# Latent attention of a fused two-block network: the former item's values ahead of this item's turns, ScalarE's copy between the two exponentials, the first low part at the tenth item

## The chip, the cores and the metric

One core of a Trainium2 chip. The time is device microseconds (us) for one execution of the whole program. TensorE (PE) multiplies and transposes into PSUM, VectorE (DVE) and ScalarE (ACT) read PSUM and SBUF, GpSimd (POOL) works on SBUF, and SyncE (SP) issues most transfers. Each engine runs its own list of instructions in order and waits on semaphores for the others.

## The reference

Two blocks work on 512 tokens of width 1024. The first block has two layers; each of them projects the normed input, runs a latent attention and a dilated attention, gates both, and adds a product with `w_out`. The second block has a feed-forward part, a recurrence with a banded attention, and another feed-forward part. The change lies in the latent attention, once in each of the two layers:

```python
q = (rms_norm(c_q, q_norm_g) @ w_uq).reshape(B, S, 8, 64 + 32)      # nope | rope
kv = (rms_norm(c_kv, kv_norm_g) @ w_ukv).reshape(B, S, 8, 64 + 64)  # k_nope | v
s = (einsum('bqhd,bkhd->bhqk', qn, k_nope) + einsum('bqhr,bkr->bhqk', qr, k_rope)) * 96 ** -0.5
p = softmax(s, axis=-1)
a = einsum('bhqk,bkhd->bqhd', p, v) * silu(gate_a)
x = x + concatenate([a, b], axis=-1) @ w_out
```

There is no mask: 8 heads, 512 queries, 512 keys.

## The kernel before

Large products run with both operands split into a high and a low part (three matmuls at lines 1208 to 1210), so nearly all of TensorE's time is such triples. Loads, splits and products follow a plan made when the program is built (`make_plan`).

**Items.** The latent attention (`kind == "mla"`) of a layer is cut into 16 items: item n has a pair of heads j = n // 4 and a tile of 128 queries t = n % 4. `first` marks t = 0 and `last` marks t = 3. Dilated and banded attention are cut the same way (`"dil"`, `"swa"`), and share the loops. `scores(n)` on TensorE makes 10 matmuls with 64 contracted rows for two heads side by side, over 512 keys, into two PSUM banks. DVE's `maxima(n)` reduces each bank (line 2617). ACT's `exp_of_item(n, parts)` takes the exponential of each bank into `PR` and sums it (line 1948); part 0 and part 1 are the two heads. `turn(n)` on TensorE transposes the probabilities into banks 4 and 5 (32 small transposes, line 1387; the first 16 need part 0, the others part 1). DVE copies bank 4 to `PT` (line 2635) and ACT copies bank 5 (line 1973, `turned(n)`). `values(n)` multiplies `PT` with the values into bank 6 (32 matmuls with 64 weight columns, line 1419).

**Buffers.** `PR` and `PT` hold two items each; banks 4 and 5 hold one. So `turn(n)` waits until both copies of item n-1 are done (`pt_dve`, `pt_act`), and `values(n)` waits for both copies of item n.

**After a pair of heads.** Behind a last item DVE takes the reciprocals of the sums (`sums_spread`, line 2641), ACT widens them (`sums_wide`, line 2007), TensorE transposes them into bank 7 (`spread_sums`, line 1400), and DVE multiplies the gate by bank 7 (line 2650) and by the values in bank 6 (line 2653, `result`). ACT then writes the high part of this product (`hi_of_value`, line 1991, in `CATM`) and DVE the low part (`lo_of_value`, line 2664). Both are operands of the output projection that follows the attention (`wo`, the triples on `CATD` and `CATM`). DVE also stacks low parts of later heads at items 0 to 3, 6 and 7 of the stage (`stack_low`, line 2706).

**Order before.** TensorE, for the latent attention: `scores(n+1)`, `turn(n)`, `spread_sums(n-1)` where item n-1 is a last one, `values(n-1)`. For the other attentions (`ahead`): `scores(n+1)`, `values(n-1)`, `turn(n)`. ACT, latent: both exponentials of item n+1, the copy of item n, the widening, the high part. ACT, other: exponential part 0, copy, result, exponential part 1. DVE: maxima of n+1, the copy of n, stacking, reciprocals, result of n-1, and a low part at items 6, 13 and 14 of the stage. The last two items are finished inside the first output projection (`rest`), in both versions alike.

Of the kernel before, what the change touches and what calls it, by code (L numbers as in the profile page):

```python
# [360 lines left out]
def build_program(nc, a, out):  # L361

    pl = make_plan()
    ctx = ExitStack()
    with ctx:
# [827 lines left out]
        def _(pe):  # L1193
# [160 lines left out]
            def attention(name, filler):  # L1354

                n0, n1 = pl.item_at[name]
                kind = name[0]
# [34 lines left out]
                def spread_sums(n):  # L1392

                    it = pl.items[n]
                    g = 4 * it["L"] + it["j"]
                    pe.wait_ge(rl_ready, g + 1)
                    if g:
                        pe.wait_ge(gated_a, g)
                    for t in range(NT):
                        last = nc.tensor.transpose(bank(7)[:, t * P:(t + 1) * P],  # L1400
                                                   RLB[:, 2 * t:2 * t + 2, :].rearrange("p h d -> p (h d)"), IDN[:, :])
                    last.then_inc(rlt_ready, 1)

                def values(n):
                    it = pl.items[n]
                    pe.wait_ge(pt_dve, n + 1)
                    pe.wait_ge(pt_act, n + 1)
                    if it["first"]:
                        results_taken(n)
                    if n == n0:  # L1410
                        if kind == "swa":
                            pe.wait_ge(dve_out, pl.dve_out[filler_of[name]])
                        elif kind == "dil":
                            pe.wait_ge(dve_out, pl.dve_out[filler_of[name]])
                            pe.wait_ge(w0_in if it["hh"] else v0_in, 16 * 12 * (it["L"] + 1))
                        else:
                            pe.wait_ge(act_out, pl.act_out["uv", it["L"], 1])
                    for dst, k, v, start, stop in value_products(it):
                        last = nc.tensor.matmul(dst, v, turned_block(n, k), start=start, stop=stop,  # L1419
                                                skip_group_check=True)  # L1420
                    last.then_inc(pv_done, 1)
# [7 lines left out]
                for n in range(n0, n1 - 1):  # L1429
                    if n0 + 1 < n + 1 < n1:  # L1430
                        scores(n + 1)
                    if ahead and n > n0:
                        values(n - 1)
                    turn(n)
                    if not ahead and n > n0:
                        if pl.items[n - 1]["last"]:
                            spread_sums(n - 1)
                        values(n - 1)

                def rest(k):  # L1440
                    if k == (1 if ahead else 5):
# [391 lines left out]
        def _(act):  # L1833
# [103 lines left out]
            def exp_of_item(n, heads=(0, 1)):  # L1937
                it = pl.items[n]
                kind, t, j = it["kind"], it["t"], it["j"]
                for b in heads:  # L1940
                    act.wait_ge(nm_ready, 2 * n + 1 + b)
                    if n >= 2:
                        act.wait_ge(t_ready, 2 * n - 3 + b)
                    sc = bank(2 * pl.pair["item", n] + b)
                    pr = PR[:, n % 2, b * S:(b + 1) * S]
                    if kind == "mla":
                        h = 2 * j + b
                        last = nc.scalar.activation(pr, sc, ACT.Exp, bias=NMM[:, h, t:t + 1], scale=1.0,
                                                    accum_out=LSM[:, h, t:t + 1])
                    elif kind == "dil":  # L1950
                        hh, h = it["hh"], 2 * it["jj"] + b
                        nc.scalar.activation(pr[:, 0:2 * P], sc[:, 0:2 * P], ACT.Exp,
                                             bias=NAT[:, hh, 0, 0, t, h:h + 1], scale=-1.0,
                                             accum_out=NAT[:, hh, 1, 0, t, h:h + 1])
                        last = nc.scalar.activation(pr[:, 2 * P:], sc[:, 2 * P:], ACT.Exp,
                                                    bias=RES[:, hh, t, 0, h:h + 1], scale=-1.0,
                                                    accum_out=RES[:, hh, t, 1, h:h + 1])
                    else:
                        w = min(t + 1, 2) * P
                        for u in range(2):  # L1960
                            h = 4 * j + 2 * u + b
                            last = nc.scalar.activation(pr[:, u * 2 * P:u * 2 * P + w], sc[:, u * 2 * P:u * 2 * P + w],
                                                        ACT.Exp, bias=SNM[:, h, t:t + 1], scale=-1.0,
                                                        accum_out=SLS[:, h, t:t + 1])
                    last.then_inc(p_ready, 1)

            def turned(n):

                act.wait_ge(t_ready, 2 * n + 2)
                if n >= 2:  # L1970
                    act.wait_ge(pv_done, n - 1)
                it = pl.items[n]
                nc.scalar.activation(used_half(it, PT[:, n % 2, S:]), used_half(it, bank(5)), ACT.Copy
                                     ).then_inc(pt_act, 1)

            def result(it):

                act.wait_ge(pv_done, it["n"] + 1)
                dst = OUN[:, it["j"], 1, :] if it["kind"] == "dil" else OSU[:, 2 * it["j"] + 1, :]
                nc.scalar.activation(dst, bank(7), ACT.Copy).then_inc(o_act, 1)  # L1980
# [29 lines left out]
            def attention(name, filler):  # L2010
                n0, n1 = pl.item_at[name]
                mla = name[0] == "mla"
                if not mla:
                    table(ACT.Exp)
                exp_of_item(n0)
                exp_of_item(n0 + 1)
                filler()
                for n in range(n0, n1):
                    more = n0 + 1 < n + 1 < n1
                    if more:  # L2020
                        exp_of_item(n + 1, (0, 1) if mla else (0,))
                    turned(n)
                    if mla and pl.items[n]["last"]:
                        sums_wide(pl.items[n])
                    if n > n0 and pl.items[n - 1]["last"] and not mla:
                        result(pl.items[n - 1])
                    if more and not mla:
                        exp_of_item(n + 1, (1,))
                    if n > n0 + 1 and pl.items[n - 2]["last"] and mla:
                        hi_of_value(("mla", name[1], pl.items[n - 2]["j"]))  # L2030
                if mla:
                    hi_of_value(("mla", name[1], HEADS // 2 - 1))
                else:
                    result(pl.items[n1 - 1])
                act.wait_ge(w_hi, pl.chunk[filler_of[name]] + 3)
# [412 lines left out]
        def _(dve):  # L2448
# [210 lines left out]
            def lo_of_value(key):  # L2659

                kind, L, j = key
                dve.wait_ge(cat_hi, pl.val[key])
                cat, src = (CATM, GA) if kind == "mla" else (CATD, GB)
                tt(cat[:, j, 1, :], src[:, j, :], cat[:, j, 0, :].bitcast(F32), ALU.subtract).then_inc(cat_lo, 1)
# [45 lines left out]
            def attention(name, filler=None):  # L2710
                n0, n1 = pl.item_at[name]
                mla = name[0] == "mla"
                maxima(n0)
                maxima(n0 + 1)
                if filler:
                    filler()
                for n in range(n0, n1):
                    it = pl.items[n]
                    if n0 + 1 < n + 1 < n1:
                        maxima(n + 1)  # L2720
                    turned(n)
                    if mla and heads_to_stack(name, n):
                        stack_low(name, heads_to_stack(name, n))
                    if mla and it["last"]:
                        sums_spread(it)
                    if n > n0 and pl.items[n - 1]["last"]:
                        result(pl.items[n - 1])
                    if mla and n - n0 in (6, 13, 14):
                        lo_of_value(("mla", name[1], (6, 13, 14).index(n - n0)))
                result(pl.items[n1 - 1])  # L2730
                if mla:
                    lo_of_value(("mla", name[1], HEADS // 2 - 1))
                dve.wait_ge(w_split, pl.chunk[filler_of[name]] + 3)
# [679 lines left out]
```

## Time and profile before

| what | value |
|---|---|
| median of 3 runs | 2043.9 us (2043.89 to 2044.02) |
| profiled execution, its own time | 2043.58 us |
| its span in the trace | 2041.8 us |
| PE busy | 2022.4 us, 99% |
| DVE, ACT, POOL busy | 1323.6, 911.6, 130.2 us |
| latent attention, layer 1, steady part | 363.97 to 407.92 us of the span |
| latent attention, layer 2, steady part | 806.27 to 850.23 us of the span |

The steady part runs from the start of the scores of item 2 to the start of the output projection. The profiled execution took 1.8 us more than its span, which lies around the first and last recorded instruction. A line of the timeline has the start of a group of like instructions, how long the group lasted, engine, line of the kernel, operation, destination and sources, shape and count; in brackets stands idle time ahead of it. Matmuls are pipelined: the start of the next group tells more than the length of one.

### The profile page before, as it was taken

The page shows a single profiled execution, that of the slowest core. Times are in us where ns is not written, and L with a number is a line of the kernel's source. Part 1 is how long each engine was busy: PE and PEld are TensorE (multiplying, and loading weights), DVE is VectorE, ACT ScalarE, POOL GpSimd, SP SyncE. Part 2 cuts the span into 40 slices and gives each one's busy share as a digit, 9 for nine tenths or more (in the row PEclk, how much of TensorE's full clock was granted, in tenths as well). Part 3 has the DMA queues.
Part 4 walks back from the last instruction along what each step waited for, and adds up shares of the span by engine and source line. Part 5 has one row for each costly group of instructions (what it writes and reads, how often), then busy time and mean ns, then how long its engine had stood idle before and what let it go on. Part 6 is the DMA issues. An engine that isn't in the chain of part 4 may idle for free.

```text
span 2041.8 us, 31282 instructions
## 1 busy us (share of the span) xinstructions
PE 2022.4 (99%) x13047; PEld 1720.3 (84%) x13047; DVE 1323.6 (65%) x1784; ACT 911.6 (45%) x1444; POOL 130.2 (6%) x127
## 2 busy tenths in 40 slices
PE   9999999999999999999999999999999999999998
PEld 7888878788888877789999888787788888999987
DVE  6456478845556577667898547786653437898633
ACT  5252245733151436545545437464632247545423
POOL 0110010400010101300000001001000001000001
PEclk9999999999999999999999999999999999999999
DMA  6332322123313311132332233334023323242321
GB/s 196 114 94 62 103 64 86 43 63 102 109 59 88 120 45 63 43 124 83 92 116 83 104 133 106 102 117 131 22 82 103 100 86 114 83 125 83 104 103 62
DMA packets 158832, 189.49 MB, mean 93 GB/s; under 512 B 4386, under 2 KB 148836, under 8 KB 158564
## 3 DMA queue, kind: packets, MB, share of 16 engines
q1 hardware_dynamic: 155092, 176.51, 27.4%
q0 software_dynamic: 3424, 10.90, 1.7%
q8 instruction: 104, 1.70, 0.4%
q14 instruction: 36, 0.29, 0.0%
q10 hardware_dynamic: 176, 0.07, 0.0%
HBM read 182.20 MB, written 7.36 MB: 93 GB/s over the span
## 4 chain that ended last, share of the span: by engine, by line
PE 95%; DVE 3%; ACT 1%; issue 1%; DMA 0%; DVEq 0%; SPq 0%; ACTq 0%
PE PS L1208 27%; PE PS L1210 26%; PE PS L1209 26%; PE PS L1419 4%; PE PS L1371 3%; PE PS L1387 2%; PE PS L1220 1%; PE PS L1216 1%; PE PS L1217 1%; DVE PT L2635 1%; PE PS L1315 1%; PE PS L1582 0%; PE PS L1656 0%; DVE QRS L2706 0%; PE PS L1344 0%
## 5 line engine op out<-in xcount | busy, mean ns | idle before, releaser
L1208 PE MATMUL PS<-UH,WH 128*128 128x512 f32 (+1 forms) x1472 | 533.8, 363 | 0.9 <-DVE UL L3067 0.9
L1210 PE MATMUL PS<-UH,WL 128*128 128x512 f32 (+1 forms) x1472 | 527.4, 358 | 0.0
L1209 PE MATMUL PS<-UL,WH 128*128 128x512 f32 (+1 forms) x1472 | 527.3, 358 | 0.0
L1861 ACT ACTIVATE WH<-WS 128x2048 fp32r<-128x2048 f32 x104 | 199.6, 1919 | 612.5 <-PE PS L1210 588.8
L2481 DVE TENSOR_TENSOR WL<-WS,WH 128x2048 fp32r<-128x2048 f32 x104 | 238.0, 2289 | 257.4 <-ACT WH L1861 257.3
L1208 PEld LDWEIGHTS PS<-UH,WH 128*128 128x128 f32 x1472 | 278.2, 189 | 47.2 <-issue 6.1
L1210 PEld LDWEIGHTS PS<-UH,WL 128*128 128x128 f32 x1472 | 278.2, 189 | 41.1
L1209 PEld LDWEIGHTS PS<-UL,WH 128*128 128x128 f32 x1472 | 278.4, 189 | 38.6
L1419 PE MATMUL PS<-PT,ARENA 128*64 128x128 f32 x1248 | 85.8, 279 | 7.6 <-DVE PT L2635 2.7
L1419 PEld LDWEIGHTS PS<-PT,ARENA 128*64 128x64 f32 x1248 | 67.0, 136 | 22.7 <-DVE PT L2635 13.6
L1208 PE MATMUL PS<-WH,UH 128*128 128x512 f32 (+1 forms) x224 | 84.0, 375 | 0.2 <-issue 0.2
L1209 PE MATMUL PS<-WL,UH 128*128 128x512 f32 (+1 forms) x224 | 83.8, 374 | 0.0
L1210 PE MATMUL PS<-WH,UL 128*128 128x512 f32 (+1 forms) x224 | 83.8, 374 | 0.0
L1208 PE MATMUL PS<-S12H,WH 128*128 128x256 f32 x288 | 81.5, 283 | 0.0
L1209 PE MATMUL PS<-S12L,WH 128*128 128x256 f32 x288 | 81.5, 283 | 0.0
L1210 PE MATMUL PS<-S12H,WL 128*128 128x256 f32 x288 | 81.5, 283 | 0.0
L1208 PE MATMUL PS<-S34Hf,WH 128*128 128x256 f32 x288 | 81.5, 283 | 0.0
L1209 PE MATMUL PS<-S34Lf,WH 128*128 128x256 f32 x288 | 81.5, 283 | 0.0
L1210 PE MATMUL PS<-S34Hf,WL 128*128 128x256 f32 x288 | 81.5, 283 | 0.0
L2088 ACT ACTIVATE WH<-RAW 128x1024 fp32r<-128x1024 f32 x60 | 63.2, 1055 | 37.2 <-PE PS L1210 37.2
L2814 DVE TENSOR_TENSOR WL<-RAW,WH 128x1024 fp32r<-128x1024 f32 x60 | 73.0, 1220 | 8.1 <-ACT WH L2088 8.1
L2635 DVE COPY PT<-PS 128x512 f32<-128x512 f32 (+1 forms) x80 | 53.9, 673 | 26.7 <-PE PS L1387 25.6
(393 smaller groups left out, 4070.9 us busy)
## 6 DMA issues: line engine op xcount, KB each, us to landing
WS<-in_w_in SPq DMA_DIRECT2D x50, 1024.0 KB, 5.3
WS<-in_ffn_w SPq DMA_DIRECT2D x46, 1024.0 KB, 5.3
RAW<-in_ffn_w SPq DMA_DIRECT2D x20, 1024.0 KB, 7.9
WS<-in_w_in SPq DMA_DIRECT2D x22, 512.0 KB, 4.4
WS<-in_w_out SPq DMA_DIRECT2D x8, 1024.0 KB, 5.1
WS<-in_w_gate SPq DMA_DIRECT2D x8, 1024.0 KB, 5.4
WS<-in_w_attn_out SPq DMA_DIRECT2D x4, 1024.0 KB, 5.1
WS<-in_w_lru_out SPq DMA_DIRECT2D x4, 1024.0 KB, 5.0
```

The lines of the kernel that those rows point to most:

```text
L1208: nc.tensor.matmul(dst, sh, mh, start=start, stop=False, skip_group_check=True)
L1209: nc.tensor.matmul(dst, sh, ml, start=False, stop=False, skip_group_check=True)
L1210: return nc.tensor.matmul(dst, sl, mh, start=False, stop=stop, skip_group_check=True)
L1216: nc.tensor.matmul(dst, sh, mh, start=start, stop=False, skip_group_check=True)
L1371: last[b] = nc.tensor.matmul(acc[:, c0:c0 + w], q, k, start=start, stop=True, skip_group_check=True)
L1387: last = nc.tensor.transpose(turned_half(bank(4 + r), 4 * b + k), PR[rows_of(r), n % 2, b * S + k * P:b * S + (k + 1) * P], IDN[rows_of(r) ...
L1419: last = nc.tensor.matmul(dst, v, turned_block(n, k), start=start, stop=stop, skip_group_check=True)
L1861: nc.scalar.activation(WH[:, c % 2, 0:kt * n], staged(c, kt * n), ACT.Copy).then_inc(w_hi, 1)
L2088: nc.scalar.activation(group_slot(WH, f, g), group_source(i, j), ACT.Copy).then_inc(grp_hi, 1)
L2481: tt(WL[:, c % 2, 0:kt * n], staged(c, kt * n), WH[:, c % 2, 0:kt * n].bitcast(F32), ALU.subtract).then_inc(w_split, 1)
L2635: nc.vector.tensor_copy(used_half(it, PT[:, n % 2, 0:S]), used_half(it, bank(4))).then_inc(pt_dve, 1)
L2814: tt(group_slot(WL, f, g), group_source(i, j), group_slot(WH, f, g).bitcast(F32), ALU.subtract).then_inc(grp_lo, 1)
```

## The change

On TensorE the latent attention takes the order of the other two: `values(n-1)` ahead of `turn(n)`, with `spread_sums(n-1)` behind `turn(n)`. On ACT the copy of item n stands between part 0 and part 1 of the exponentials of item n+1, and the widening behind part 1. On DVE the first low part of a layer stands at the tenth item (9) where it stood at the seventh (6). The other attentions keep their order.

```diff
                 for n in range(n0, n1 - 1):
                     if n0 + 1 < n + 1 < n1:
                         scores(n + 1)
-                    if ahead and n > n0:
+                    if n > n0:
                         values(n - 1)
                     turn(n)
-                    if not ahead and n > n0:
-                        if pl.items[n - 1]["last"]:
-                            spread_sums(n - 1)
-                        values(n - 1)
+                    if kind == "mla" and n > n0 and pl.items[n - 1]["last"]:
+                        spread_sums(n - 1)
...
                     if more:
-                        exp_of_item(n + 1, (0, 1) if mla else (0,))
+                        exp_of_item(n + 1, (0,))
                     turned(n)
+                    if n > n0 and pl.items[n - 1]["last"] and not mla:
+                        result(pl.items[n - 1])
+                    if more:
+                        exp_of_item(n + 1, (1,))
                     if mla and pl.items[n]["last"]:
                         sums_wide(pl.items[n])
-                    if n > n0 and pl.items[n - 1]["last"] and not mla:
-                        result(pl.items[n - 1])
-                    if more and not mla:
-                        exp_of_item(n + 1, (1,))
...
-                    if mla and n - n0 in (6, 13, 14):
-                        lo_of_value(("mla", name[1], (6, 13, 14).index(n - n0)))
+                    if mla and n - n0 in (9, 13, 14):
+                        lo_of_value(("mla", name[1], (9, 13, 14).index(n - n0)))
```

## Rows read from the trace of the kernel before

**Rows 1.** The page: span, and TensorE's busy time.

```profile
span 2041.8 us, 31282 instructions
...
PE 2022.4 (99%) x13047; PEld 1720.3 (84%) x13047; DVE 1323.6 (65%) x1784; ACT 911.6 (45%) x1444; POOL 130.2 (6%) x127
```

**Rows 2.** Busy time by window, the steady part of both layers.

```profile
363.97:407.92 43.95, 43.36 (x608) 34.01 (x603) 36.53 (x60) 30.31 (x76) 18.42 (x12) 1.00 0.15 50
806.27:850.23 43.96, 43.37 (x608) 34.00 (x603) 36.56 (x60) 30.34 (x76) 18.41 (x12) 1.00 0.16 50
```

**Rows 3.** Timeline of PE, two items of the first layer.

```profile
366.83 0.73 PE L1371 MATMUL PS<-KRS,QRS 64*128 64x512 f32 x4
...
368.27 0.71 PE L1387 MATMUL PS<-IDN,PR 64*128 64x64 f32 x16
...
369.94 0.73 PE L1371 MATMUL PS<-KRS,QRS 64*128 64x512 f32 x4
...
370.97 0.40 PE L1371 MATMUL PS<-KNH,QNL 64*128 64x512 f32 x2
371.20 0.66 PE L1387 MATMUL PS<-IDN,PR 64*128 64x64 f32 x16
371.79 1.09 PE L1419 MATMUL PS<-PT,ARENA 128*64 128x128 f32 x16
372.81 0.73 PE L1371 MATMUL PS<-KRS,QRS 64*128 64x512 f32 x4
```

**Rows 4.** Timeline of ACT at the same items.

```profile
367.58 0.59 ACT L1973 ACTIVATE PT<-PS 128x512 f32<-128x512 f32 x1
...
372.13 0.69 ACT L1948 ACTIVATE PR<-PS,NMM 128x512 f32<-128x512 f32 x1 [1.17 <-DVE NMM L2617]
```

**Rows 5.** Timeline of PE at item 8, the longest gap.

```profile
387.22 0.71 PE L1387 MATMUL PS<-IDN,PR 64*128 64x64 f32 x16 [0.41 <-issue]
388.02 0.66 PE L1400 MATMUL PS<-IDN,ARENA 128*128 128x128 f32 x4
388.61 1.09 PE L1419 MATMUL PS<-PT,ARENA 128*64 128x128 f32 x16
```

**Rows 6.** Timeline of ACT ahead of that gap.

```profile
386.53 0.59 ACT L1973 ACTIVATE PT<-PS 128x512 f32<-128x512 f32 x1
```

**Rows 7.** Timeline of DVE: low part, maxima after item 9, last copy.

```profile
383.56 0.99 DVE L2664 TENSOR_TENSOR CATM<-ARENA,CATM 128x512 fp32r<-128x512 f32 x1
...
393.99 1.29 DVE L2617 TENSOR_REDUCE NMM<-PS 128x1 f32<-128x512 f32 x2 [1.00 <-PE PS L1371]
...
411.28 0.69 DVE L2635 COPY PT<-PS 128x512 f32<-128x512 f32 x1 [2.41 <-PE PS L1387]
```

**Rows 8.** Timeline of PE where groups follow in other orders.

```profile
138.43 1.09 PE L1419 MATMUL PS<-PT,ARENA 128*64 128x128 f32 x16 [0.32 <-DVE PT L2635]
...
142.07 0.71 PE L1387 MATMUL PS<-IDN,PR 64*128 64x64 f32 x16
142.62 1.11 PE L1371 MATMUL PS<-ARENA 64*128 64x128 f32 x16
...
360.14 0.41 PE L1371 MATMUL PS<-KNH,QNL 64*128 64x512 f32 x2
360.48 0.50 PE L1208 MATMUL PS<-WH,CH 128*128 128x512 f32 x1
...
363.45 0.72 PE L1387 MATMUL PS<-IDN,PR 64*128 64x64 f32 x16
363.97 0.71 PE L1371 MATMUL PS<-KRS,QRS 64*128 64x512 f32 x4
...
364.98 0.41 PE L1371 MATMUL PS<-KNH,QNL 64*128 64x512 f32 x2
...
410.52 0.71 PE L1387 MATMUL PS<-IDN,PR 64*128 64x64 f32 x16
411.17 0.50 PE L1208 MATMUL PS<-CATD,WH 128*128 128x512 f32 x1
```

## The prediction, made before the changed kernel was run

> **What bounds the kernel now.** I read the page first, then the windows of the latent attention, then the timelines of TensorE, ACT and DVE in it. TensorE is busy for 2022.4 of 2041.8 us [rows 1]. No other engine bounds the whole, so the change can only give back time in which TensorE stands between two groups in the latent attention, and it can only cost time by making TensorE stand or by a dearer order of its own groups. The two stages are alike: 43.95 and 43.96 us, with the clock granted in full [rows 2]. A stage holds 14 rounds of scores, turns and values, and three times the transposes that spread the sums.
>
> The reader is to see in [rows 3] that the rounds differ. The scores at 369.94 are followed by turns at 371.20, values at 371.79 and the next scores at 372.81: 1.26 + 0.59 + 1.02 = 2.87 us, and nothing was waited for. The round at 366.83 has the same work, but its turns began at 368.27, 1.44 us behind the scores, and the next scores at 369.94, 3.11 us behind them. The turns wait for ACT's copy of the former item: that copy began at 367.58 and lasted 0.59, so it ended at 368.17, 0.10 ahead of the turns [rows 3, 4]. It stood in the queue behind both exponentials of the coming item, and those start late: scores at 369.94, exponential at 372.13, 2.19 later [rows 3, 4]. Every second round waits like this, because a round that waited gives the next one slack. Item 8 is the worst. The turns at 387.22 have 0.41 idle ahead of them [rows 5], and again ACT's copy ended 0.10 before, at 386.53 + 0.59 = 387.12 [rows 6]. There DVE had the low part of the first pair, 0.99 long, ahead of the maxima of this item [rows 7].
>
> What all of this costs in a stage is the stage's time less the rounds without waiting. Fourteen rounds of 2.87 are 40.18. The three spreads add turns to a 128-row group, 0.65 (410.52 to 411.17) [rows 8], plus the spread itself, 0.59 (388.02 to 388.61) [rows 5], in place of the 0.59 from turns to values, so 0.65 each, 1.95. Together 42.13, and 43.95 - 42.13 = 1.8 us per stage is waiting.
>
> **The change, part by part.**
>
> ACT's copy between the exponentials. Nothing is added: the same instructions in another order. The copy of item n now stands behind one exponential. The copy comes earlier, and the part 1 exponential ends about 0.6 later; only the second half of the turns wants it. With the round of the next paragraph, count from the start of scores(n+1). Exponential part 0 starts at 2.19 [rows 3, 4], and takes some 0.7 with its sum. The turns of item n start at 1.35 + 1.02 = 2.37, and a copy starts 0.76 behind the start of its turns (410.52 to 411.28) [rows 7, 8], so at 3.13, after the exponential. ACT's copy ends at 3.72, part 1 ends near 4.4, and the turns that want it start at 2.90 + 2.37 = 5.27. Cover is 0.9 us. If it were gone, each round would lengthen by what is missing.
>
> Values ahead of turns. This moves 32 matmuls of each of 14 rounds ahead of 32 transposes. The wait for the former copies, which stood in front of the turns, now stands in front of the values, behind the same scores; what is queued behind it is the turns, and behind them the next scores, on which DVE's maxima wait. Between the turns of an item and the values of the same item only one group of scores lies now, where there were values and scores. The copies have 0.53 + 1.35 = 1.88 us from the start of the turns. DVE's copy is there at 0.76 + 0.69 = 1.45, plus the 0.10 seen above, 1.55. Slack is about 0.3. DVE's maxima do not stand in its way: they end at about 2.7 by the count above, before 3.13. On the items on which DVE stacks a low part (0.69) or takes a result (twice 0.69) it is late for the maxima by some tenths, and the copy still waits for the turns. So I cost new waits at nothing, with a slack of 0.3 as the cover.
>
> The order has a price of its own, which no row shows as a whole, since the latent attention never ran this way before. I take it from neighbours.
> - Turns to scores: 0.52 (363.45 to 363.97), and 0.55 in the dilated attention, which has this order (142.07 to 142.62) [rows 8]. I take 0.53; the row nearest is the first, the same scores, but its turns stood behind another group.
> - Scores after turns: 1.01 to their last pair (363.97 to 364.98) [rows 8], against 1.03 after values (369.94 to 370.97) [rows 3].
> - Last pair of scores to values: unseen. To turns it is 0.23 (370.97 to 371.20) [rows 3], to a group over all 128 rows 0.34 (360.14 to 360.48) [rows 8]. I take 0.34, since values use all 128 rows too. The bounds are 0.23 below and 0.45 above, the latter with the extra 0.11 taken twice, since values change the columns of a tile as well as its rows.
> - Values: 1.02 [rows 3].
>
> A round is then 1.35 + 1.02 + 0.53 = 2.90, against 2.87 without waits and 3.11 with one. A stage is 14 x 2.37 = 33.18 for scores and values, ten steps from turns to scores 5.30, three spreads of 0.65 + 0.59 = 3.72, and one step from turns to the output projection, 0.65: 42.85 us. It was 43.95. The saving is 1.1 us per stage: 1.8 of waits given back, 0.7 paid for the order.
>
> At this point a rule bears. The row shows the step from 64-row scores to a 128-row group at 0.34, against 0.23 where the next group is 64-row too [rows 3, 8]. The Trainium skill, "TensorEngine Tiling (Array Packing)", section "Tiling Modes", Key Properties, says that changing the tiling mode drains the engine. The trace agrees in direction: 0.11 more at such a step. A round has two such changes in either order, so by that rule with one price per change the order is free. The rule's own result is the first rival below.
>
> The first low part from item 6 to item 9. The same instruction, 0.69 to 0.99 long, in each layer. At item 6 it delayed the maxima of item 8, which ended as the 0.41 of idle TensorE; this is inside the 1.8. At item 9 DVE stood idle for 1.00 ahead of its next maxima [rows 7], which covers it. With less cover in the new order the maxima come up to 0.4 late, and ACT's copy behind part 0 up to 0.3 late, which uses up the slack of that one item. What it costs if not covered is 0.3 per layer. Its reader is the output projection, far behind. No DMA is issued by a moved step; GpSimd's splits of the coming weights wait for DVE's copy of item 8 and move with the stage.
>
> Start and end of a stage: the turns of item 0 start at 363.45 [rows 8] and its values would start 0.52 + 1.35 = 1.87 later, the same slack as in any round. The end (`rest`) keeps its order.
>
> **Sum.** Two stages give 2 x 1.1 = 2.2 us. The profiled execution took 2043.6; less 2.2 is 2041.4. The median of the runs shown is 0.3 above that execution, so 2041.7 us.
>
> **The rivals.**
> - The order is free: each change between groups costs the same in either order. Then the whole 1.8 comes back twice, 3.6 us: 2043.9 - 3.6 = 2040.3. For it: two changes in either round. Against: the 0.34 of [rows 8]. Chance 0.14.
> - The step from scores to values is as cheap as to turns (0.23). The stage then saves another 14 x 0.11 = 1.5, two stages 3.1: 2043.9 - 2.2 - 3.1 = 2038.6, which is faster by 0.26%. Against: no 128-row group in the trace follows so closely. Chance 0.09.
> - The waiting stays, because it is set by the exponentials and not by the place of the copy. Then only the order's price is left, 2 x 0.7: 2045.3, and with part of it, near no change. Against: the copy ended 0.10 ahead of each late turn. Chance 0.10, half of it above 2044.0.
> - Slower: values wait for the copies of their own item. The dilated attention, which has this order, waited so once for 0.32 at 138.43 [rows 8], behind shorter scores. It decides once the copies end more than 0.3 later than worked out. At 0.32 in all 28 rounds it costs 9.0: 2043.9 - 2.2 + 9.0 = 2050.7. If only the items with stacked low parts wait, 12 x 0.3 = 3.6 leaves 2045.3. Chance of the first 0.04, of the second 0.03.
> - The forecast, waits gone and 0.7 per stage paid: 0.60, by itself 2040.8 to 2042.6.
>
> **How the numbers follow.** What can be told from no change is about 0.2%, 4.1 us, so faster is below 2039.8 and slower above 2048.0. Faster holds the cheap step and the low edge of the free order: 0.11. Slower holds the full wait on the copies: 0.05. The rest, 0.84, is within. The range runs from 2039.9, just under the free order, to 2044.0, which takes in half of the waiting that stays and the bound of the scores step (0.45 in place of 0.34 costs 2 x 14 x 0.11 = 3.1: 2044.8) but for its last 0.8. It leaves out the cheap step and the slow cases, about 0.2.
>
> **What would show it.** In the changed profile: the steady part of both stages near 42.9 us; turns start 1.02 behind values; scores start 0.52 to 0.55 behind turns; values start 0.34 behind the last pair of scores, and all rounds are alike, near 2.90, not long and short in turn. No idle near item 8. ACT's copy starts about 0.76 behind its turns. The prediction is wrong if TensorE shows idle time ahead of the values released by a copy, if scores to values is 0.23 or 0.45, or if the gain of the stage is lost again in the output projection behind it.

## The result and the profile after

The changed kernel takes 2049.8 us (median of 8 runs) where the kernel before takes 2044.0 in the same runs: ratio 1.0027, 95% interval 1.0018 to 1.0036. It is 5.8 us slower. The forecast was 2041.7, within a range of 2039.9 to 2044.0.

The page of the changed kernel answers to [rows 1]. The span is longer by 6.8, and TensorE is busy for only 2.4 more, so it is mostly waiting that grew. Lines behind the changed places stand two lower in this kernel: 1971 is ScalarE's copy (1973 before), 2615 DVE's maxima (2617), 2651 DVE's product with bank 6 (2653), 2662 the low part (2664).

```profile
span 2048.6 us, 31282 instructions
...
PE 2024.8 (99%) x13047; PEld 1721.3 (84%) x13047; DVE 1330.3 (65%) x1784; ACT 913.2 (45%) x1444; POOL 129.8 (6%) x127
```

The waits of TensorE in the changed kernel, whole span: two lines carry the news. The columns are microseconds in total, times, and the longest.

```profile
PE PS L1419 <- ACT PT L1971: 4.3, 3, 2.2
...
PE PS L1419 <- DVE ARENA L2651: 2.1, 6, 0.4
```

The windows of both steady parts of the changed kernel, and of 2.9 us in the first, answer to [rows 2]. Behind the window and its length stand the busy times of TensorE, its weight loads, DVE, ACT and GpSimd; of the last three figures the first is the granted clock.

```profile
364.93:412.73 47.80, 44.53 (x607) 33.91 (x603) 39.64 (x59) 30.91 (x75) 18.17 (x12) 0.96 0.14 46
811.16:857.06 45.90, 42.99 (x607) 32.83 (x602) 39.29 (x59) 30.91 (x75) 18.18 (x12) 1.00 0.15 48
402.30:405.20 2.90, 2.90 (x26) 1.98 (x22) 1.35 (x3) 1.72 (x5) 1.75 (x1) 0.59 0.04 10
```

The stages lost 47.80 - 43.95 = 3.85 and 45.90 - 43.96 = 1.94, together 5.8, which is the difference of the medians. Between the stages nothing moved: from the end of one to the start of the other it is 811.16 - 412.73 = 398.4 in this kernel, 806.27 - 407.92 = 398.4 in the kernel before [rows 2]. The first stage starts 0.96 later than before although nothing ahead of it was changed; starts between 363.9 and 365.7 were seen in all the kernels of this study, and nothing here is read from them.

TensorE's timeline in the changed kernel answers to [rows 3]: one plain round, then the two places where rounds are long.

```profile
369.15 1.10 PE L1419 MATMUL PS<-PT,ARENA 128*64 128x128 f32 x16
370.18 0.72 PE L1387 MATMUL PS<-IDN,PR 64*128 64x64 f32 x16
370.70 0.71 PE L1371 MATMUL PS<-KRS,QRS 64*128 64x512 f32 x4
...
371.70 0.40 PE L1371 MATMUL PS<-KNH,QNL 64*128 64x512 f32 x2
372.04 1.10 PE L1419 MATMUL PS<-PT,ARENA 128*64 128x128 f32 x16
...
378.97 1.09 PE L1419 MATMUL PS<-PT,ARENA 128*64 128x128 f32 x16 [0.35 <-DVE ARENA L2651]
...
399.72 1.09 PE L1419 MATMUL PS<-PT,ARENA 128*64 128x128 f32 x16 [2.21 <-ACT PT L1971]
...
402.28 0.63 PE L1371 MATMUL PS<-KNH,QNH 64*128 64x512 f32 x2
402.70 0.63 PE L1371 MATMUL PS<-KNL,QNH 64*128 64x512 f32 x2
```

The plain round is as forecast: 1.03 from values to turns, 0.52 to scores, 1.34 to values, 2.89 in all, with the last pair of scores 0.34 ahead of the values. But values at 378.97 waited for DVE's line 2651, and those at 399.72 for 2.21 us. Behind that gap the products run at little more than half pace: 0.42 from one pair of scores to the next, where the plain round has 0.23 or 0.24.

What stands behind the long gap is on DVE, ACT and GpSimd of the changed kernel:

```profile
394.06 3.62 DVE L2662 TENSOR_TENSOR CATM<-ARENA,CATM 128x512 fp32r<-128x512 f32 x1
397.60 1.27 DVE L2615 TENSOR_REDUCE NMM<-PS 128x1 f32<-128x512 f32 x2
```

```profile
398.31 0.69 ACT L1946 ACTIVATE PR<-PS,NMM 128x512 f32<-128x512 f32 x1 [3.08 <-DVE NMM L2615]
...
398.99 0.59 ACT L1971 ACTIVATE PT<-PS 128x512 f32<-128x512 f32 x1
```

```profile
392.55 4.57 POOL L1099 TENSOR_TENSOR WL<-WS,WH 128x2048 fp32r<-128x2048 f32 x1
397.07 2.36 POOL L1096 CAST WH<-WS 128x2048 fp32r<-128x2048 f32 x1
```

The chain is to be read from the top. The moved low part took 3.62 where its fellows take 0.68. The maxima of item 11 are queued behind it, ACT's exponential behind the maxima, ACT's copy behind the exponential (it had been ready to copy since the turns), and TensorE's values behind the copy. GpSimd began its subtraction 1.5 us ahead of the low part and ended it at 392.55 + 4.57 = 397.12; the low part ended at 394.06 + 3.62 = 397.68, 0.56 later. A long bar of DVE is not work here: the time it was held is shown as its own duration, not as idle time.

### The profile page after: what moved, and what is told of

Read it like the earlier page. It is cut to its first block, busy times and chain, and to the rows that moved or that the text cites. A ratio compares the mean times of both kernels' runs of the same rounds, so it can differ in the third digit from the quotient of the medians.

```text
span 2048.6 us, 31282 instructions
## 1 busy us (share of the span) xinstructions
PE 2024.8 (99%) x13047; PEld 1721.3 (84%) x13047; DVE 1330.3 (65%) x1784; ACT 913.2 (45%) x1444; POOL 129.8 (6%) x127
## 4 chain that ended last, share of the span: by engine, by line
PE 94%; DVE 3%; issue 1%; ACT 1%; DMA 0%; DVEq 0%; ACTq 0%
PE PS L1208 27%; PE PS L1210 26%; PE PS L1209 26%; PE PS L1419 4%; PE PS L1371 3%; PE PS L1387 2%; PE PS L1220 1%; PE PS L1216 1%; PE PS L1217 1%; PE PS L1315 1%; DVE PT L2633 0%; PE PS L1580 0%; PE PS L1654 0%; PE PS L1344 0%; DVE QNL L3137 0%
```

## The experiments

The eight kernels ran in two groups of four, each group on one chip together with the kernel before, whose median was 2044.2 in the first group (a_lo6, b_lo9, b_act, b_pe) and 2045.0 in the second. The medians are given with the ratio to the kernel before of the same group. Since the start of the program varies by about a microsecond, and nothing outside the stages moves in most of them, the steady parts of the stages are the sharper measure.

| kernel | us | ratio, 95% interval | stage 1 | stage 2 |
|---|---|---|---|---|
| before | 2044.0, 2044.2 and 2045.0 | | 43.95 | 43.96 |
| changed | 2049.8 | 1.0027 (1.0018 to 1.0036) | 47.80 | 45.90 |
| a_lo6 | 2045.3 | 1.0005 (0.9996 to 1.0014) | 44.39 | 44.40 |
| b_lo9 | 2049.6 | 1.0026 (1.0015 to 1.0038) | 46.02 | 47.13 |
| b_act | 2043.6 | 0.9996 (0.9987 to 1.0005) | 43.29 | 43.28 |
| b_pe | 2047.1 | 1.0013 (1.0004 to 1.0022) | 45.42 | 45.42 |
| b_best | 2041.9 | 0.9986 (0.9977 to 0.9994) | 42.57 | 42.53 |
| a_late | 2050.4 | 1.0028 (1.0017 to 1.0039) | 43.99 | 44.00 |
| a_copy | 2046.0 (one run) | | 43.99 | 45.06 |
| a_free | 2041.5 | 0.9985 (0.9976 to 0.9994) | 42.70 | 42.70 |

**a_lo6: the changed kernel without the move of the low part.**

```diff
-                    if mla and n - n0 in (9, 13, 14):
-                        lo_of_value(("mla", name[1], (9, 13, 14).index(n - n0)))
+                    if mla and n - n0 in (6, 13, 14):
+                        lo_of_value(("mla", name[1], (6, 13, 14).index(n - n0)))
```

> The changed kernel with the first low part put back to item 6. Theory A (DVE's low part at item 9 runs beside GpSimd's subtraction of two SBUF operands and is held until that ends, 3.6 us in place of 0.7; all of the loss hangs on this): the low part takes 0.7 to 1.0, no idle time ahead of the values of item 9, no stretch at the low clock, each stage falls from 47.8 to about 44.0 us, and the time is 2043.9 +-0.7. Theory B (the new order of TensorE costs the time, and the long low part is only a bystander): the idle time moves to another group of values and the time stays above 2047.

The windows of a_lo6:

```profile
365.00:409.39 44.39, 43.00 (x607) 32.84 (x602) 36.90 (x59) 31.11 (x75) 17.75 (x12) 1.00 0.15 50
807.70:852.10 44.40, 43.00 (x608) 32.86 (x602) 36.90 (x59) 31.12 (x75) 17.73 (x12) 1.00 0.15 49
```

The long gap and the low clock are gone, and the time is 0.05% above before, no difference that can be told. That is theory A. The median of 2045.3 is outside the 0.7 that I allowed, but single runs of before in this group reach 2045.5. The stages are 0.44 longer than before, so the two new orders by themselves gain nothing as they stand. Most of the 0.44 is item 8, whose round takes 3.99 here and 3.60 in the changed kernel: the low part at item 6 still delays it, though it takes only 0.69.

**b_lo9: the kernel before with only the low part moved.**

```diff
-                    if mla and n - n0 in (6, 13, 14):
-                        lo_of_value(("mla", name[1], (6, 13, 14).index(n - n0)))
+                    if mla and n - n0 in (9, 13, 14):
+                        lo_of_value(("mla", name[1], (9, 13, 14).index(n - n0)))
```

> The kernel before with nothing changed but the first low part, at item 9. Theory A: the low part takes over 3 us here too, because GpSimd's subtraction lies there in both orders; about 2 us of idle time ahead of a group of turns in each stage, 0.6 given back at item 8, so 1.4 lost per stage: 2046.7, and up to 2050 if the clock falls as well. Theory B: the low part fits in the 1.00 that DVE had idle, the wait at item 8 goes, 2042.8.

The windows of b_lo9, the third of them 3.4 us in the second stage:

```profile
363.91:409.93 46.02, 43.33 (x607) 34.00 (x603) 39.50 (x60) 30.30 (x76) 18.85 (x12) 1.00 0.15 48
808.28:855.41 47.13, 44.79 (x608) 35.08 (x602) 39.11 (x60) 30.27 (x76) 18.85 (x12) 0.96 0.14 46
844.30:847.70 3.40, 3.40 (x30) 2.52 (x28) 0.61 (x3) 0.83 (x2) 2.29 (x1) 0.51 0.04 6
```

And from its timeline, DVE, GpSimd and TensorE of the first stage:

```profile
392.30 3.91 DVE L2664 TENSOR_TENSOR CATM<-ARENA,CATM 128x512 fp32r<-128x512 f32 x1
...
391.09 4.57 POOL L1099 TENSOR_TENSOR WL<-WS,WH 128x2048 fp32r<-128x2048 f32 x1
...
398.87 0.71 PE L1387 MATMUL PS<-IDN,PR 64*128 64x64 f32 x16 [2.52 <-ACT PT L1973]
```

This edit alone gives a loss as large as the whole change does, 2049.6. The third window has the clock at 0.51 behind a gap like this one. The low part ends at 396.21, GpSimd's subtraction at 395.66, 0.55 apart. Theory A had 2046.7 and up to 2050 with the clock; it was the clock's case, in the second stage here. Theory B (2042.8) falls.

**b_act: the kernel before with ScalarE's order alone.**

```diff
-                        exp_of_item(n + 1, (0, 1) if mla else (0,))
+                        exp_of_item(n + 1, (0,))
                     turned(n)
+                    if n > n0 and pl.items[n - 1]["last"] and not mla:
+                        result(pl.items[n - 1])
+                    if more:
+                        exp_of_item(n + 1, (1,))
                     if mla and pl.items[n]["last"]:
                         sums_wide(pl.items[n])
-                    if n > n0 and pl.items[n - 1]["last"] and not mla:
-                        result(pl.items[n - 1])
-                    if more and not mla:
-                        exp_of_item(n + 1, (1,))
```

> The kernel before with ScalarE's new order alone. Both theories have the long and short rounds end, since the late turns waited for this copy: 1.3 to 1.8 us per stage, time 2040.4 to 2041.3. If instead the waiting is set by the exponentials, nothing changes: 2043.9.

One window of b_act, and TensorE at item 8:

```profile
365.27:408.56 43.29, 42.55 (x608) 34.40 (x603) 36.39 (x60) 30.18 (x76) 18.43 (x12) 1.00 0.16 51
```

```profile
388.23 0.46 PE L1387 MATMUL PS<-IDN,PR 64*128 64x64 f32 x8 [0.16 <-ACT PR L1948]
```

The late turns waited for this copy: apart from the rounds of the pairs' ends, all rounds are now between 2.86 and 2.89. But the stage saves 0.66 and not 1.3 to 1.8, because the round of item 8 did not shrink: it grew from 4.27 to 4.44. The turns there are split: their second half waits for exponential part 1, which is now behind the copy, and the spread of the sums behind them waits 0.38 for ACT's widening. Ahead of both DVE's low part at item 6 took 1.00. The time, 0.9996, can't be told from before.

**b_pe: the kernel before with TensorE's order alone.**

```diff
-                    if ahead and n > n0:
+                    if n > n0:
                         values(n - 1)
                     turn(n)
-                    if not ahead and n > n0:
-                        if pl.items[n - 1]["last"]:
-                            spread_sums(n - 1)
-                        values(n - 1)
+                    if kind == "mla" and n > n0 and pl.items[n - 1]["last"]:
+                        spread_sums(n - 1)
```

> The kernel before with TensorE's new order alone; ScalarE still copies behind both exponentials. Theory A: by the count of the prediction the copy ends about when values want it, a few tenths of waiting at most in some rounds, and at the first item of each pair of heads values wait 0.4 for DVE's product with bank 6 (three times per stage): 2044 to 2046, the low part below 1.0. Theory B: over 2047, as the order is the cause.

One window of b_pe, and TensorE at item 8:

```profile
364.48:409.90 45.42, 43.25 (x608) 32.90 (x603) 36.82 (x59) 30.41 (x76) 17.75 (x12) 1.00 0.15 49
```

```profile
388.58 1.09 PE L1419 MATMUL PS<-PT,ARENA 128*64 128x128 f32 x16 [0.97 <-ACT PT L1971]
```

It is slower by 0.13%, 2.9 us, more than theory A's upper bound of 2046 and just over theory B's 2047. The stage has 1.5 more than before: three rounds of 3.33 (the wait of 0.35 for DVE's product that frees bank 6, and the step behind it), and 0.97 of idle time at item 8 behind ACT's copy, which still follows two exponentials. So the order of TensorE costs time of its own, though not the 5.8 us, and it leans on ScalarE's new order: with both, a_lo6, the stage is 1.0 shorter.

**b_best: ScalarE's order, and the low parts after GpSimd's work.** The order of TensorE is that of before.

```diff
 (on b_act)
-                    if mla and n - n0 in (6, 13, 14):
-                        lo_of_value(("mla", name[1], (6, 13, 14).index(n - n0)))
+                    if mla and n - n0 in (13, 14, 15):
+                        lo_of_value(("mla", name[1], (13, 14, 15).index(n - n0)))
```

> The kernel before with ScalarE's new order, and the low parts at items 13, 14 and 15, after GpSimd's last work of the stage. Theory A (the low part is held by GpSimd; in the run with ScalarE's order alone the round of item 8 was the only long one left, 4.44 us, behind the low part at item 6 beside GpSimd's casts): no low part over 0.75, the round of item 8 falls to 3.5, a stage takes 42.3 us where before took 43.95, 3.2 less in two stages. Theory B (the round of item 8 is long for the stacked low part and the reciprocals alone): it stays at 4.4 and the stage at 43.3.

Its windows:

```profile
364.15:406.72 42.57, 42.14 (x607) 34.37 (x603) 35.61 (x59) 30.25 (x76) 18.44 (x12) 1.00 0.16 52
805.07:847.60 42.53, 42.11 (x606) 34.33 (x602) 35.61 (x59) 30.25 (x76) 18.44 (x12) 1.00 0.16 51
```

All eight low parts take 0.64 to 0.69. The round of item 8 falls to 3.75, not to 3.5: a wait of 0.20 to 0.23 for ACT's widening is left at two of the three pair ends of a stage. The stage is 42.55 where theory A had 42.3 and theory B 43.3, 1.4 less than before; the kernel is faster by 0.14%.

**a_late: the changed kernel, GpSimd two items later.** If GpSimd's subtraction is what holds the low part, moving GpSimd must free item 9, and hold whatever low part it now meets.

```diff
-                    pool.wait_ge(pt_dve, pl.item_at[name][0] + 9)
+                    pool.wait_ge(pt_dve, pl.item_at[name][0] + 11)
```

> The changed kernel, low part at item 9 as it stands there, but GpSimd starts on the coming weights behind the copy of item 10 instead of item 8. Theory A: GpSimd has nothing under way when the low part of item 9 comes, so it takes 0.7; the stage falls from 47.8 and 45.9 to about 44.0, or somewhat more if the low parts at items 13 and 14 now meet the later subtraction. Theory B (item 9 is a bad place whatever GpSimd does, as DVE has no time there): the gap ahead of the values of item 9 stays near 2 us.

One window of a_late, then low parts on DVE, GpSimd's second subtraction, and TensorE's values of item 14, which lie in the output projection:

```profile
365.66:409.65 43.99, 42.93 (x607) 32.81 (x603) 37.19 (x57) 30.34 (x73) 16.14 (x12) 1.00 0.08 26
```

```profile
394.79 0.68 DVE L2662 TENSOR_TENSOR CATM<-ARENA,CATM 128x512 fp32r<-128x512 f32 x1
...
407.49 4.33 DVE L2662 TENSOR_TENSOR CATM<-ARENA,CATM 128x512 fp32r<-128x512 f32 x1
...
406.68 4.59 POOL L1099 TENSOR_TENSOR WL<-WS,WH 128x2048 fp32r<-128x2048 f32 x1
...
413.86 1.10 PE L1419 MATMUL PS<-PT,ARENA 128*64 128x128 f32 x16 [2.56 <-ACT PT L1971]
```

And of the second layer TensorE's values of item 14, and a window behind them:

```profile
858.51 1.09 PE L1419 MATMUL PS<-PT,ARENA 128*64 128x128 f32 x16 [2.22 <-ACT PT L1971]
...
860.00:864.00 4.00, 4.00 (x24) 3.21 (x21) 0.80 (x2) 1.23 (x2) 0.00 (x0) 0.63 0.08 26
```

The low part of item 9, at the same place in the program, takes 0.68, and both steady parts fall to 44.0, the count of theory A. The one of item 13 now meets the second subtraction, takes 4.33 and ends 0.55 behind it. The gap of 2.56 us went with it, out of the window, and so did the one of the second layer, 2.22 with a granted clock of 0.63 in the 4 us behind it, so the whole kernel is as slow as the changed one. Item 9 was no bad place; the meeting was bad.

**a_copy: the changed kernel with GpSimd's subtraction made a plain copy.** It leaves the subtraction out for two chunks of weights per layer, and it ran once, so only its trace is read.

```diff
+                    if name[0] == "mla":
+                        nc.gpsimd.tensor_copy(WL[:, c % 2, :], WS[:, c % 2, :]).then_inc(w_split, 1)
+                        continue
                     nc.gpsimd.tensor_tensor(WL[:, c % 2, :], WS[:, c % 2, :], WH[:, c % 2, :].bitcast(F32),
                                             ALU.subtract).then_inc(w_split, 1)
```

> The changed kernel, with GpSimd's subtraction of the two operands in the latent attention replaced by a plain copy of the weights into the low half, so the low parts of two weight chunks per layer are wrong. Theory A1 (any GpSimd instruction that reads SBUF holds the low part until it ends): the low part at item 9 ends about 0.55 behind the end of the GpSimd copy of 1.9 us that it meets, so it takes up to 2.4 and not 3.6. Theory A2 (only a subtraction with two operands holds it): 0.7.

The low part at item 9 and what GpSimd had under way, first stage and second:

```profile
394.26 0.92 DVE L2665 TENSOR_TENSOR CATM<-ARENA,CATM 128x512 fp32r<-128x512 f32 x1
...
836.60 2.40 DVE L2665 TENSOR_TENSOR CATM<-ARENA,CATM 128x512 fp32r<-128x512 f32 x1
```

```profile
392.73 1.90 POOL L1100 CAST WL<-WS 128x2048 fp32r<-128x2048 f32 x1
...
836.56 1.90 POOL L1096 CAST WH<-WS 128x2048 fp32r<-128x2048 f32 x1
```

A copy holds the low part just as well. In the first stage GpSimd's copy ended at 394.63 and the low part at 395.18, in the second 838.46 and 839.00: 0.55 and 0.54. The hold of the first (0.24 over 0.68) cost TensorE nothing, stage 43.99; that of the second (1.7) cost 1.00 of idle time, stage 45.06. So DVE can be late by some tenths at item 9 and not by two microseconds, and theory A2 falls.

**a_free: TensorE's and ScalarE's new orders, with TensorE's waits taken away.**

```diff
 (on a_lo6; low parts at 13, 14, 15)
-                    dve.wait_ge(rlt_ready, g + 1)
                     dve.wait_ge(gate_a_ready, it["L"] + 1)
-                    tt(GA[:, j, :], GA[:, j, :], bank(7), ALU.mult).then_inc(gated_a, 1)
-                    dve.wait_ge(gated_a, g + 1)
                     dve.wait_ge(pv_done, n + 1)
-                    tt(GA[:, j, :], GA[:, j, :], bank(6), ALU.mult).then_inc(o_dve, 1)
+                    tt(GA[:, j, :], GA[:, j, :], bank(6), ALU.mult).then_inc(gated_a, 1)
+                    dve.wait_ge(gated_a, g + 1)
+                    dve.wait_ge(rlt_ready, g + 1)
+                    tt(GA[:, j, :], GA[:, j, :], bank(7), ALU.mult).then_inc(o_dve, 1)
...
-                    if g:
-                        pe.wait_ge(gated_a, g)
+                    if it["j"]:
+                        pe.wait_ge(o_dve, it["o_dve"] - 1)
...
-                    if it["first"]:
+                    if kind == "mla" and it["first"] and n > n0:
+                        pe.wait_ge(gated_a, 4 * it["L"] + it["j"])
+                    elif it["first"]:
                         results_taken(n)
```

> TensorE's and ScalarE's new orders, the low parts at items 13, 14 and 15, and in DVE's result the product with bank 6 ahead of the one with bank 7, with TensorE's values of a first item waiting only for the former. Theory A: the 0.44 of waiting at each of three rounds per stage goes, and the low part's 0.4 at item 8; rounds of 2.89 and 3.60 alone, stage 42.7, 1.3 less than before, 2.5 in all. That the order itself costs 0.4 to 0.7 per stage shows against the run that keeps TensorE's old order. Theory C (the new order is free once its waits are gone): the stage comes to 42.3 or less, like that run.

Its windows, in which TensorE has no idle time at all:

```profile
364.36:407.06 42.70, 42.70 (x608) 32.64 (x603) 36.39 (x58) 31.15 (x75) 17.78 (x12) 1.00 0.16 51
805.38:848.08 42.70, 42.70 (x608) 32.64 (x603) 36.39 (x58) 31.15 (x75) 17.77 (x12) 1.00 0.16 51
```

As counted, 42.7. Both a_free and b_best are faster than the kernel before (0.15% and 0.14%), and they can't be told from each other. Against b_best the plain rounds are 2.88 to 2.90 in place of 2.87 and the step to the output projection costs 0.14 more, which is the order's price; in return the spread of the sums is never waited for, which makes two of the three rounds at a pair's end 3.60 in place of 3.75 (the third is 3.60 in place of 3.46).

## Why the prediction was wrong, point by point

**The step that failed.** "At item 9 DVE stood idle for 1.00 ahead of its next maxima [rows 7], which covers it. ... What it costs if not covered is 0.3 per layer." I took the low part at 0.69 to 0.99 long wherever it stands, and did not look at GpSimd, whose subtraction of 4.57 us lies over item 9 in the kernel before as well. I looked at DVE's slack on its own queue only. The low part took 3.62 and 3.25 there, and TensorE stood 2.21 us in the first stage. b_lo9 shows that this edit alone makes the loss, a_lo6 that without it there is none, and a_late that it goes where GpSimd's work goes. The 0.99 of [rows 7] was the sign: a row of four casts of GpSimd ran from 381.05 to 384.02, the low part began at 383.56 while the fourth was under way, and it ended at 384.55, 0.53 behind it, like all the others. I read a wait as a duration.

GpSimd in the kernel before, the casts at item 6 and the subtraction over item 9, and the same casts one by one (shortest, median and longest in ns, starts of the first and the last):

```profile
381.05 2.97 POOL L1145 CAST QRS<-QRH 32x512 fp32r<-32x512 f32 x4 [9.65 <-PE PS L1371]
...
391.51 4.57 POOL L1099 TENSOR_TENSOR WL<-WS,WH 128x2048 fp32r<-128x2048 f32 x1
...
L1145 POOL CAST QRS<-QRH x4: 604/608/957, 381.0 to 383.1; 32x512 fp32r<-32x512 f32 x4
```

The trace also had a sign that the prediction names for itself: TensorE's idle time ahead of the values at item 9 is released by a copy. With the low part out of the way the forecast would still have failed, by the new waits of the first items (below): a stage of 44.0 in place of 42.85.

The Trainium skill states it, in "SBUF — State Buffer", section "SBUF: two separate sides": DVE and GpSimd share one pair of ports as an exclusive lock; a DVE instruction with two SBUF inputs and a GpSimd instruction that reads SBUF exclude each other for the whole length of the one that came first. The traces agree in all twelve meetings of a first low part or of a_late's second one with GpSimd (two each in before, changed, b_lo9, b_act, a_late and a_copy), with 0.53 to 0.56 from GpSimd's end to DVE's, and the other way round with GpSimd's cast of 1.89 that took 2.36 when the low part was just running out. They agree on the other half too: maxima and copies, which read PSUM, kept their 1.27 to 1.29 and 0.67 to 0.69 beside GpSimd, and so did DVE's products of one SBUF operand with a PSUM bank beside GpSimd's subtraction in a_late (0.68 and 0.69 at 403.44 and 404.15, GpSimd from 400.20 to 404.77).

**Slower, but by no rival of mine.** The slow rival had values waiting for the copies of their own item in all rounds, or at the items with stacked low parts, because the copies come too late in the order itself. In the trace the plain rounds wait for nothing. The waiting at item 9 does come through a copy, but from behind a held instruction in one round of fourteen.

**The clock.** Behind the gap of 2.21 us the first stage ran at the lower level for a stretch: the granted clock is 0.59 on average from 402.30 to 405.20, so it was at 1.2 GHz for most of it. The rounds of items 10 and 11 took 5.18 and 5.12, in the second stage, where the clock held, 4.79 and 3.60. That is the 1.90 between the two stages: 0.37 of it is the longer gap (2.21 against 1.84), and the other 1.5 the clock. I had no term for it, as I forecast no gap.

**The first items of a pair.** "I cost new waits at nothing" failed a second time. Values of a first item overwrite bank 6 and so wait for DVE's product with it. Before, that product had a whole group of turns and one of values more. Now values come 0.35 too soon, and a round that should take 2.89 takes 3.33, three times a stage: 1.3 us, 2.6 in both. I had worked out where DVE's result lies, and only asked whether it delays DVE's next maxima. b_pe and a_lo6 have this wait too, and a_free, which orders the two products the other way, is without it: its stage is 1.3 shorter than a_late's, which has these waits and no others.

**What was right.** The 1.8 us of waiting per stage were there, and a_free, in which TensorE has no idle time, is without them. They were not all waits for ACT's copy: b_act, which moves the copy alone, has no plain round that waits and gives 0.66; the low part moved away from item 6 gives 0.74 more (43.29 to 42.55); the rest is in the spread of the sums, where b_best still waits 0.20 and 0.23 for ACT's widening. The price of the order was forecast at 2.90 for a plain round and 42.85 for a stage; a_free, which runs it without waits, has 2.88 to 2.90 and 42.70. The step from scores to values was 0.34, the neighbour's value, so the rival with 0.23 falls. The free order falls as well: it had 3.6 us in all, and a_free gives 2 x 1.25 = 2.5. The rival in which the waiting stays, set by the exponentials, falls for the plain rounds and holds in part at item 8, where b_act's turns wait 0.16 for the second exponential in place of the copy.

**The sum as it should have been.** Waits given back and the order paid, -1.25 per stage; three first items, +1.3; hence 44.0, as the steady part of a_late shows, and no change from 43.95. The held low part, +1.9 in the second stage; in the first +3.8, with a longer gap and 1.5 of lower clock. Together +5.8.

## What to carry to other kernels

Before an instruction is moved into an idle place of its engine, look at what the other engines do there: VectorE and GpSimd exclude each other where VectorE reads two operands from SBUF and GpSimd reads SBUF too, and the trace shows the hold as a longer instruction, so an instruction that takes 0.99 where its fellows take 0.68 is a wait to be explained. When a consumer is moved ahead, list everything that it waits for, the release of the bank that it overwrites too, and count each from its own engine. A gap of two microseconds on TensorE may cost more than its length, once as idle time and once as clock (3.8 for a gap of 2.21 in the first stage here, 1.9 for one of 1.84 in the second).

## What the runs showed of the hardware that I had not expected

The hold is total and ends alike each time: DVE's subtraction of 512 columns finished 0.53 to 0.56 us behind GpSimd's instruction, whether that was a subtraction of 4.57 us, a copy of 1.90, or the last of a row of short casts. That last cast in the kernel before took 0.96 where its fellows took 0.60 or 0.61: a stacking instruction of DVE with two operands in SBUF was under way until 383.53, and here it was GpSimd that stood.

Gaps of like length had unlike effects on the clock. In b_lo9 the gap of 2.52 us in the first stage left the clock at its upper level (1.00 over the stage), and the one of 2.17 in the second was followed by the stretch at the lower level. In the changed kernel it was the first stage, with 2.21, while the 1.84 of the second left the clock alone. In a_late the 2.56 of the first layer left it at 1.00, and the 2.22 of the second was followed by the lower level. So the two longest of these six gaps cost no clock, and length alone does not decide. What does, no run here shows.
